# The order of the query tiles within each pair of heads of a causal forgetting attention, on one Trainium2 core

## What is computed

```python
for blk in range(t_len // 128):
    s0 = blk * 128
    e = s0 + 128
    s = q[s0:e] @ k[:e].T * scale + log_f_cum[s0:e, None] - log_f_cum[None, :e]
    p = softmax(where(query >= key, s, -inf))
    out[s0:e] = p @ v[:e]
```

## Time and profile before

| | us |
|---|---|
| median of 3 runs | 2467.86 (2466.03 to 2472.21) |
| profiled execution | 2464.29 |
| its span | 2462.5 |
| TensorE busy | 2247.1 (91% of the span) |
| VectorE busy | 1104.6 (45%) |
| ScalarE busy | 801.8 (33%) |
| forgetting attention, first score to last subtraction | 1923.62 to 2008.3 |

### The profile page before, as it was taken

How to read it: one execution, slowest core, us unless ns; L and a number is a source line. 1 busy time by engine, 2 the same in 40 slices (tenths; PEclk the granted TensorE clock), 3 DMA queues, 4 the chain that set the end, 5 groups by cost and what they waited for, 6 DMA issues and landing times. The chain is left out here.

```text
span 2462.5 us, 27222 instructions
## 1 busy us (share of the span) xinstructions
PE 2247.1 (91%) x11000; PEld 1778.1 (72%) x11000; DVE 1104.6 (45%) x1648; ACT 801.8 (33%) x1129; POOL 209.3 (8%) x73
## 2 busy tenths in 40 slices
PE   6998899899999966999686899999899898999997
PEld 4875567688778755877585688888678566888885
DVE  2015663343253355576664544442462555444423
ACT  4311473242132133343123332221331653322211
POOL 3331002300000032320000000000000000000000
PEclk9997999999999987899888999999999998999998
DMA  3211001223222221232211122232224011232321
GB/s 124 102 60 48 1 1 69 75 96 103 86 86 97 75 77 39 69 111 87 75 45 52 64 91 103 86 103 86 86 86 171 1 50 64 93 103 86 103 86 52
DMA packets 43015, 190.21 MB, mean 77 GB/s; under 512 B 15808, under 2 KB 16512, under 8 KB 22032
## 3 DMA queue, kind: packets, MB, share of 16 engines
q1 hardware_dynamic: 40560, 184.32, 22.0%
q10 hardware_dynamic: 2336, 4.23, 0.5%
HBM read 184.80 MB, written 3.74 MB: 77 GB/s over the span
## 5 line engine op out<-in xcount | busy, mean ns | idle before, releaser
L233 DVE TENSOR_TENSOR weights_low<-weights_raw,weights_high 128x2048 fp32r<-128x2048 f32 x126 | 288.8, 2292 | 544.8 <-ACT weights_high L206 544.8
L206 ACT CAST weights_high<-weights_raw 128x2048 fp32r<-128x2048 f32 x164 | 309.7, 1889 | 587.2 <-PE psum L408 576.8
L406 PE MATMUL psum<-split,weights_high 128*128 128x512 f32 (+1 forms) x904 | 362.6, 401 | 22.8 <-DVE split L1669 18.3
L408 PE MATMUL psum<-split,weights_low 128*128 128x512 f32 (+1 forms) x904 | 362.8, 401 | 0.0
L407 PE MATMUL psum<-split,weights_high 128*128 128x512 f32 (+1 forms) x904 | 360.5, 399 | 0.0
L406 PE MATMUL psum<-block_split,weights_high 128*128 128x512 f32 (+1 forms) x608 | 246.2, 405 | 16.0 <-POOL block_split L559 5.9
L408 PE MATMUL psum<-block_split,weights_low 128*128 128x512 f32 (+1 forms) x608 | 244.0, 401 | 0.0
L407 PE MATMUL psum<-block_split,weights_high 128*128 128x512 f32 (+1 forms) x608 | 242.5, 399 | 0.0
L223 POOL TENSOR_TENSOR weights_low<-weights_raw,weights_high 128x2048 fp32r<-128x2048 f32 (+3 forms) x38 | 168.2, 4426 | 779.6 <-ACTq L1532 392.9
L406 PEld LDWEIGHTS psum<-split,weights_high 128*128 128x128 f32 (+1 forms) x904 | 171.9, 190 | 69.7 <-issue 18.4
L407 PEld LDWEIGHTS psum<-split,weights_high 128*128 128x128 f32 (+1 forms) x904 | 172.1, 190 | 42.5
(11 more groups left out here) (416 smaller groups left out, 3400.0 us busy)
## 6 DMA issues: line engine op xcount, KB each, us to landing
weights_raw<-in_weights SPq DMA_DIRECT2D x161, 1024.0 KB, 4.9
minus_c<-minus_c_rows ACTq DMA_DIRECT2D x16, 256.0 KB, 7.2
x_stream<-in_x SPq DMA_DIRECT2D x2, 1024.0 KB, 8.0
gdn_in_grown<-gdn_rows SPq DMA_DIRECT2D x4, 512.0 KB, 4.5
gdn_chain_grown<-gdn_rows SPq DMA_DIRECT2D x4, 512.0 KB, 4.0
out<-x_stream SPq DMA_DIRECT2D x8, 256.0 KB, 2.1
rope_table<-rope_tables SPq DMA_DIRECT2D x1, 1024.0 KB, 5.2
weights_raw<-in_weights SPq DMA_DIRECT2D x1, 768.0 KB, 4.2
```

The lines of the kernel that those rows point to most:

```text
L206: self.nc.scalar.copy(self.high[:, chunk.slot, 0:width], self.raw[:, chunk.slot, 0:width]).then_inc(self.high_ready, 1)
L233: self.nc.vector.tensor_tensor(out=self.low[:, n % 2, 0:width], in0=self.raw[:, n % 2, 0:width], in1=self.high[:, n % 2, 0:width].bitcast( ...
L406: nc.tensor.matmul(bank, wh, ah, start=first, stop=False)
L408: return nc.tensor.matmul(bank, wl, ah, start=False, stop=last)
```

## The change

The steps of each pair in the forgetting attention go from `qt` 3 (512 keys) down to `qt` 0 (128 keys); the attentions of the first block keep their order. Three conditions asked for the first or last tile of a pair by `qt`; they now ask by the step's place in its pair, which is the same as before where the order is not turned.

```diff
--- before.py
+++ after.py
@@ -999,7 +999,7 @@
         def attention(label, pairs, out_split, forget=False, prob=None, decayed=None):
 
 
-            steps = [(pair, qt) for pair in pairs for qt in range(TT)]
+            steps = [(pair, qt) for pair in pairs for qt in (reversed(range(TT)) if forget else range(TT))]
             units = 2 * len(steps)
             last_of_pair = TT - 1
             with stage(label) as s:
@@ -1056,7 +1056,7 @@
 
                         def attend(step):
                             pair, qt = steps[step]
-                            if qt == 0 and step >= TT:
+                            if step % TT == 0 and step >= TT:
                                 pe.wait_ge(stored, step // TT)
                             for head in range(2):
                                 wait_copied(pe, 2 * step + head)
@@ -1105,7 +1105,7 @@
                         def finish(step):
 
                             pair, qt = steps[step]
-                            if qt == last_of_pair:
+                            if step % TT == last_of_pair:
                                 dve.wait_ge(high_ready, step // TT + 1)
                                 nc.vector.tensor_tensor(out=out_split[:, 1, pair.out, :], in0=psum[:, 7, :],
                                                         in1=out_split[:, 0, pair.out, :].bitcast(f32),
```

## The result

The changed kernel takes 2470.57 us (median of 22 runs, 2466.97 to 2476.35) against 2466.66 us for the kernel before on the same chips (22 runs, 2462.8 to 2472.21). The ratio is 1.0017, with an interval from 1.0010 to 1.0024: about 4 us slower, inside the 0.3% that I had called no change, but told from zero. I had forecast +1.9 us.

The account below looks back on a forecast made before the run. TensorE was taken to set the forgetting attention's pace; start +1.5, six pairs +2.7 and end -2.3 gave +1.9 us on 2467.86, so 2469.8 us, range 2465.5 to 2476.

Parts of the forecast that it names:

- boundary wait: TensorE's wait at a pair's end, before the transposes of the 3-block tile: 1.60 us; with its second head, 0.85 grows to 1.65.
- other wait: TensorE's second wait per pair: old 0.52 us gone, none before tile 2's transposes, 0.17 us before the next tile 4's.
- six pairs: Stage's middle, last attend of the first pair to that of the seventh: 0.45 us more per pair, +2.7 us.
- tail: Stage's end, from the seventh pair's last attend to the last subtraction: 7.71 us instead of 10.03, -2.3 us.
- head: Stage's start, from first score to the first pair's last attend: 14.24 us instead of 12.78, +1.5 (+0.8 to +2.2).
- the stretch at a granted clock of 0.50, 3.4 us long: In the stage's start: TensorE at 1.2 GHz instead of 2.4, costing up to 1.7 us where it is busy.
- Rival 2: Clock falls at all seven inner pair ends, up to 1.7 us each: 2481.7 us; slower; chance 0.10, 0.07 with four or more.
- the forecast's own last sentence: In the changed profile, a pair of 10.2 us or less, or mid-stage granted clock below 1.00, would make the forecast wrong.
- Rival 1: Waits balance out: pair stays near 10.2 to 10.3 us, shorter stage end outweighs its start, 2467 to 2468 us; chance 0.20.
- Rival 3: Waits vanish: all 1.37 us per pair goes at eight pairs, -11 us, 2457 us; chance 0.02.

## Why the prediction was right, and where it was not

- **The boundary wait** was right in mechanism and size: 1.62 us, laid out as 1.60, with the cast held by the copies of tile 4. Moving the subtraction took it away in both orders and left the turned order no slower than the other; lengthening the chain by 0.48 brought the old order's pair to 10.69, near the turned order's 10.73.
- **The other wait**: 0.18 for 0.17, and none for tile 2. The seconds inside the turns of tiles 3 and 4 were 0.05 each; I had counted one of them. A pair is 8.83 + 1.62 + 0.18 + 0.10 = 10.73, forecast 10.65. For six pairs +3.2 us, forecast +2.7.
- **The tail**: 7.81 us, forecast 7.71; -2.2 for -2.3.
- **The head** was mis-sized: +3.3 us for +1.5, and outside my bounds (0.8 to 2.2). I had the work right, but took the half clock to last 3.4 us as in the earlier trace rows. It lasts 6.8 in both profiles of this order, which costs up to 1.7 more. The step that failed is "the stretch at a granted clock of 0.50, 3.4 us long": I carried the clock of one order over to another. Why it lasts longer stays open.
- **Rival 2, the clock**, had a chance of 0.10. It came in part: one fall in each of the two profiles of the changed kernel, +1.6 us, where it needed four to turn the sign by more than 0.3%. My argument against it, that the new pause is shorter than the 1.9 us that brought no fall, was wrong: in the old order with the doubled cast, pauses of 1.08 us brought two. The rule of the Trainium skill's page "TensorE: Matmul & The Clock Gate", section "A second HAM failure mode: psum-queue depth-cycling", that brief and frequent idling makes the clock swing, is borne out by one pair in seven, at a pause of 1.46 us, and not by the others. By the forecast's own last sentence a granted clock below 1.00 in the middle of the stage speaks against it, and this fall is one.
- **What the sum left out**: the stages behind. From the last subtraction to the end of the span they take 452.3 us instead of 454.8 (452.4 and 454.8 in the second profiles). The next stage's half clock at its start, 3.4 us before, is gone in both profiles of the changed kernel: from the last subtraction to the matmuls of L1765 it is 49.73 us instead of 51.28, and these matmuls then take 1.16 instead of 2.08, again for the clock. The two places make 2.5 us. In sum: head +3.3, pairs +3.2, fall +1.6, tail -2.2, later stages -2.5 is +3.4, beside the 3.9 measured between the medians. The rest of the difference between the two profiled spans, 5.6 us, lies ahead of the stage (first score at 1929.18 for 1923.62), where the two kernels have the same instructions, and is the execution's: the second profile of the changed kernel had 1922.04.
- **Rival 1** (waits balance out) fell with the pair of 10.73. **Rival 3** fell as the change stood, but it named what was to be had: with the late subtraction and tiles 2-3-1-4 all 1.37 us of waits go.

So the forecast of no change held, its sign was right and its size half of what came. The errors of the head (1.8 us) and of the fall inside the stage (1.6) come from the clock and lie on the same side; the stages behind gave 2.5 of them back, also by the clock. I foresaw neither, so that the total came within 2 us of the forecast is in part luck; the boundary wait and the tail are not.

## What to carry to other kernels

When steps of unequal size go through in-order engines, the order does not change the work, so look for the chain that must pass between two steps and add up what the bounding engine has to do meanwhile. A schedule laid out from one traced pair gave every pair of this study to about 0.1 us. A tail operation that waits for another engine belongs behind the work that the bounding engine waits for next, here the subtraction behind the normalisation. Repair that place first, and then choose the order: without the repair the orders took 9.70 to 10.73 us per pair; with it 1-2-3-4 and 4-3-2-1 are 0.07 apart, and 2-3-1-4, which has neither wait, is 0.6 below both.

## What the runs showed of the hardware

Pauses of TensorE of 1.1 to 1.95 us, once per pair, went with falls of its clock to 1.2 GHz for 3.4 us, at 1.5 to 1.6 us each, but most pauses brought none: all six profiles with such pauses had one to three falls inside the stage, and the eight in which none recurred had none. Lengthening the pause of the old order from 0.59 to 1.08 us was enough to bring two. The fall was in the seventh pair in both profiles of the changed kernel; in the two profiles of the kernel with the old first pair it was in the fifth and in the fourth, and the clock had fallen at different moments at the start. Repeated pauses of up to 0.7 us brought none in any profile here. And a stage moves the falls of the stages behind it: the one at the start of the next stage was there in both profiles of the instructions of before, and in neither of the changed kernel.
